# Feed-forward gate and value projections of one transformer layer as Strassen block products of seven terms

## What is computed

```python
def conv_ffn(h, P):
    u = depthwise_conv(h @ P['ffn_w_gate'], P['ffn_conv_w'], P['ffn_conv_b'])
    return (jax.nn.gelu(u, approximate=True) * (h @ P['ffn_w_val'])) @ P['ffn_w_down']

h = modulate(rms_norm(x, norm_ffn_pre[l]), sh2, sc2)     # h * (1 + scale) + shift
x = x + g2 * rms_norm(conv_ffn(h, P), norm_ffn_post[l])
```

## Time and profile before

| | us |
|---|---|
| median of 3 runs | 3854.72 (3853.71 to 3860.74) |
| the profiled execution | 3853.66 |
| its span, first to last instruction | 3851.9 |
| PE busy | 3631.2 (94%) |
| DVE busy | 1285.0 (33%) |
| ACT busy | 532.1 (14%) |

### The profile page before, as it was taken

The page is one execution under the profiler, slowest core; times in us unless marked ns, Lnnn a source line. Parts: engine busy times, 40 slices in busy tenths (PEclk is TensorE's granted clock), DMA queues, the critical chain, the costliest instruction groups (busy, mean ns, idle before and its releaser), DMA issues.

```text
span 3851.9 us, 43075 instructions
## 1 busy us (share of the span) xinstructions
PE 3631.2 (94%) x18490; PEld 2873.8 (75%) x18490; DVE 1285.0 (33%) x1928; ACT 532.1 (14%) x917; POOL 161.1 (4%) x166
## 2 busy tenths in 40 slices
PE   6999999978889899998999999999899979999979
PEld 2445475547778788887888888888788858888858
DVE  2257932236567410114212221000171251171260
ACT  1000012233344210010000000000101120101120
POOL 0000020000000100000000000000050000140000
PEclk9999999988889999999999999999899979999989
DMA  8868542013322434443444444444243303344303
GB/s 339 335 279 338 229 151 77 33 44 82 79 74 55 164 143 151 173 150 120 153 152 152 149 148 151 153 153 142 99 153 142 131 31 139 115 153 142 120 33 131
DMA packets 134143, 554.75 MB, mean 144 GB/s; under 512 B 57440, under 2 KB 61792, under 8 KB 72048
## 3 DMA queue, kind: packets, MB, share of 16 engines
q1 hardware_dynamic: 119680, 451.98, 33.6%
q10 hardware_dynamic: 14304, 100.42, 6.6%
HBM read 535.05 MB, written 17.30 MB: 143 GB/s over the span
## 4 chain that ended last, share of the span: by engine, by line
PE 69%; DVE 4%; ACT 2%; SPq 1%; DMA 1%; issue 1%; DVEq 0%; ACTq 0%
PE ps L435 58%; PE ps L1562 2%; PE ps L2819 1%; PE ps L1565 1%; PE ps L1660 1%; SPq L1383 1%; DVE arena L2007 1%; DVE arena L2009 1%; PE ps L2580 0%; DMA pack_t<-arena 0%; SPq L1386 0%; PE ps L2827 0%; PE ps L1439 0%; PE ps L1605 0%; PE ps L2575 0%
## 5 line engine op out<-in xcount | busy, mean ns | idle before, releaser
L435 PE MATMUL ps<-arena,ring 128*128 128x256 f32 (+3 forms) x11200 | 2586.4, 394 | 36.3 <-issue 15.7
L435 PEld LDWEIGHTS ps<-arena,ring 128*128 128x128 f32 (+1 forms) x11200 | 2136.4, 191 | 483.4 <-issue 189.7
L766 DVE SCALAR_TENSOR_TENSOR arena<-arena,small 128x512 f32<-128x512 f32 x240 | 180.4, 752 | 36.9 <-DMA arena<-in_ada_late 20.4
L2322 DVE TENSOR_TENSOR arena<-ps,arena 128x1024 f32<-128x1024 f32 x12 | 14.3, 1220 | 395.1 <-ACT arena L2308 395.1
L2699 DVE SCALAR_TENSOR_TENSOR arena<-arena,col 128x255 f32<-128x255 f32 (+29 forms) x180 | 108.2, 601 | 6.4
L570 PE MATMUL ps<-arena 128*128 128x512 f32 (+1 forms) x224 | 93.2, 565 | 5.3 <-ACT arena L631 5.3
L2443 DVE TENSOR_TENSOR arena<-ps,arena 128x1024 f32<-128x1024 f32 x11 | 13.5, 1224 | 239.2 <-PE ps L435 239.0
L2422 ACT ACT_TABLE_LOAD x11 | 14.1, 1283 | 535.0 <-DVE arena L2456 535.0
L2707 POOL TENSOR_TENSOR arena<-arena 128x1024 f32<-128x1024 f32 x2 | 4.7, 2350 | 1977.7 <-ACT arena L2648 1977.7
L570 PEld LDWEIGHTS ps<-arena 128*128 128x128 f32 x224 | 42.8, 199 | 56.3 <-issue 54.9
L1562 PE MATMUL ps<-arena 128*128 128x256 f32 x320 | 81.6, 411 | 1.0 <-ACT arena L1773 1.0
(11 more groups left out here) (419 smaller groups left out, 2969.1 us busy)
## 6 DMA issues: line engine op xcount, KB each, us to landing
ring<-in_weights SPq DMA_DIRECT2D x398, 1024.0 KB, 4.8
arena<-in_ada_late ACTq DMA_DIRECT2D x64, 1024.0 KB, 7.8
arena<-in_gates SPq DMA_DIRECT2D x56, 256.0 KB, 3.3
arena<-in_front ACTq DMA_DIRECT2D x8, 1024.0 KB, 8.9
arena<-in_x ACTq DMA_DIRECT2D x2, 2048.0 KB, 12.6
keep_g<-arena SPq DMA_DIRECT2D x14, 256.0 KB, 2.0
arena<-keep_h SPq DMA_DIRECT2D x3, 1024.0 KB, 7.8
arena<-in_ctx ACTq DMA_DIRECT2D x1, 2048.0 KB, 23.8
```

The costliest lines, as they stand in the source:

```text
L435: mm = M.matmul(o, ring[:, slot, k, c0:c0 + w], rhs, start=(kc == 0), stop=(kc == ktiles * WK - 1))
L766: ins = V.scalar_tensor_tensor(part[:, b], late[:, s, k], c, part[:, b], ALU.mult, ALU.add)
```

## The change

The first block of 512 gate and 512 value columns stays as it was, with 257 moving columns. The other ten blocks change.

Each weight tile of theirs now holds all 2048 inner rows of 128 output columns (`_chunk_tiles`), so two tiles are a matrix of 2048 x 256, which is cut in four quadrants: A11 and A12 (columns 0 to 127, rows 0 to 1023 and 1024 to 2047), A21 and A22 (the same of columns 128 to 255). The normalised input `h2` is cut in four as well: B11, B12 (tokens 0 to 127 and 128 to 255 of the first 1024 features), B21, B22. In place of the eight products of quadrants, seven are made (a form of Strassen's identity) of 8 matmuls with 128 moving columns each. A block of 512 gate and 512 value columns is four such pairs of tiles ("tile pairs" below), numbered 0 to 3: 0 and 1 are gate, 2 and 3 value; tile pairs take the PSUM halves in turn. That is 4 x 7 x 8 = 224 matmuls for each block, where 128 were.

- Once, before the loop: VectorE multiplies `hs` by `rs2` into `h2` (four instructions), ScalarE adds the shift (16 instructions), VectorE makes T1 to T4, the sums of quadrants of `h2`, and TensorE waits for T4 (`t_in4`) before its loop.
- For every tile pair VectorE makes S1 to S4 of the weights' quadrants (`weight_sums`: four instructions of 128x1024, after waiting for both tiles), in one of two buffers; TensorE waits for them (`s_in`) after its first three products, which use weights as they are.
- After every tile pair ScalarE copies the first product out of PSUM (`first_product`), and VectorE adds the products up to four quarters of the result (`quarters`: three instructions of 128x256 and one of 128x128), the last of which frees the PSUM half. This replaces the multiplication by `rs2` and the addition of the shift.
- `slot_left` is counted up at the first matmul of the first product (the second tile of the tile pair before is left) and at the first that reads S1 (the first tile of this one is left).
- The taps, the gelu and the gated product stay, from within the new order on VectorE.

```diff
+    gate, val = a['ffn_w_gate'][0], a['ffn_w_val'][0]
+    out += [_tiles(gate[:, 0:512]), _tiles(val[:, 0:512])]
+    gate, val = _chunk_tiles(gate[:, 512:]), _chunk_tiles(val[:, 512:])
...
+def _chunk_tiles(w):
+
+    return w.reshape(DC, P, -1, P).transpose(2, 1, 0, 3).reshape(-1, P, TILE)
...
+        HD = DC // 2
+        h2 = view(8192, DC, T)
...
+        PAIRS = 4
...
+        def pair_pe(p, half):
+
+            p.wait_ge(bf.free[half].sem, bf.free[half].due(p))
+            X, Y = ps[:, 4 * half], ps[:, 4 * half + 1]
+            S1, S2, S3, S4 = (S_SET[half][:, n] for n in range(4))
+
+            def product(o, w, x):
+                for k in range(HD):
+                    mm = M.matmul(o, w[:, k], x(k), start=(k == 0), stop=(k == HD - 1))
+                    if k == 0:
+                        first = mm
+                return first, mm
+            A11, A12 = quadrants(take_tile(p))
+            product(X[:, 0:P], A11, lambda k: h2[:, k, 0:P])[0].then_inc(slot_left.sem, slot_left.up(p))
+            product(X[:, P:2 * P], A12, lambda k: h2[:, HD + k, 0:P])
+            A21, A22 = quadrants(take_tile(p))
+            product(Y[:, 3 * P:4 * P], A22, lambda k: T4[:, k])
+            p.wait_ge(s_in.sem, s_in.due(p))
+            product(Y[:, 0:P], S1, lambda k: T1[:, k])[0].then_inc(slot_left.sem, slot_left.up(p))
+            product(Y[:, P:2 * P], S3, lambda k: T3[:, k])
+            product(X[:, 2 * P:3 * P], S2, lambda k: T2[:, k])
+            product(X[:, 3 * P:4 * P], S4, lambda k: h2[:, HD + k, P:T])[1].then_inc(bf.full[half].sem, bf.full[half].up(p))
+
         def ffn_pe(p):
...
-            pairs(p, FB - 1, 4, moving, bf)
+            p.wait_ge(t_in4.sem, 1)
...
+            with turns(p, FB - 1, {**per_tiles(2 * PAIRS), **bf.per(2), s_in: PAIRS}):
+                for j in range(PAIRS):
+                    pair_pe(p, j % 2)
...
+            def first_product(half):
+                a.wait_ge(bf.full[half].sem, bf.full[half].due(a))
+                S.copy(p1[:, half], ps[:, 4 * half, 0:P]).then_inc(p1_in.sem, p1_in.up(a))
...
+                first_product(0)
+                first_product(1)
+                gelus(i + 1)
+                first_product(0)
+                first_product(1)
             out_act(a)
...
+            def weight_sums(half):
+                a, b = ((ff_first[0] + 2 * half + n) % SLOTS for n in range(2))
+                for slot in (a, b):
+                    v.wait_ge(filled[slot].sem, filled[slot].due(v, 16))
+                (A11, A12), (A21, A22) = quadrants(a), quadrants(b)
+                S1, S2, S3, S4 = (S_SET[half][:, n] for n in range(4))
+                V.tensor_tensor(S1, A21, A22, ALU.add).then_inc(dve_step.sem, dve_step.up(v))
+                step(V.tensor_tensor(S3, A11, A21, ALU.subtract))
+                step(V.tensor_tensor(S2, S1, A11, ALU.subtract))
+                V.tensor_tensor(S4, A12, S2, ALU.subtract).then_inc(s_in.sem, s_in.up(v))
+
+            def quarters(dst, n, half):
...
+                v.wait_ge(p1_in.sem, p1_in.due(v))
+                step(V.tensor_tensor(q[:, 0:4:3], two(p1[:, half]), bank(0)[:, 1:3], ALU.add))
+                step(V.tensor_tensor(q[:, 1:3], two(q[:, 3]), bank(1)[:, 0:2], ALU.add))
+                V.tensor_tensor(q[:, 3], q[:, 2], bank(1)[:, 0], ALU.add).then_inc(dve_step.sem, dve_step.up(v))
                 v.wait_ge(dve_step.sem, dve_step.now(v))
...
+                step(V.tensor_tensor(q[:, 1:3], q[:, 1:3], ps[:, 4 * half:4 * half + 2, 3 * P:4 * P], ALU.add), bf.free[half])
...
+            for g in range(4):
+                V.tensor_tensor(h2[:, 4 * g:4 * g + 4], hs[:, 4 * g:4 * g + 4, 0:T], over(rs2, 4, T), ALU.mult)\
+                    .then_inc(h2_scaled.sem, h2_scaled.up(v))
+            whole(u, 0)
+            taps(0)
+            v.wait_ge(h2_in.sem, 1)
...
+            V.tensor_tensor(T4, B21, T2, ALU.subtract).then_inc(t_in4.sem, 1)
+            weight_sums(0)
+            whole(ct, 1)
+            gated(0)
+
+            def turn(i, more):
+                weight_sums(1)
+                quarters(u, 0, 0)
+                weight_sums(0)
+                quarters(u, 1, 1)
+                taps(i)
+                weight_sums(1)
+                quarters(ct, 0, 0)
+                if more:
+                    weight_sums(0)
+                quarters(ct, 1, 1)
+                gated(i)
```

More of the change, by code:

```diff
@@ L2397, in build_program, with quadrants @@
         conv_ready, gelu_ready, gv_in = again("ff_conv"), again("ff_gelu"), again("gv_in")
+        HD = DC // 2
+        h2 = view(8192, DC, T)
+        T1, T2, T3, T4 = view(13312, HD, P), view(14336, HD, P), view(15360, HD, P), view(40448, HD, P)
+        S_SET = [view(4096, 4, HD, P), view(36352, 4, HD, P)]
+        p1 = view(13056, 2, P)
+        h2_scaled, h2_in, t_in4 = again("h2_scaled"), again("h2_in"), again("t_in4")
+        s_in, p1_in = again("s_in"), again("p1_in")
+        PAIRS = 4
+        ff_first = [0]
+        def quadrants(slot):
+            w = ring[:, slot].rearrange("p k (a n) -> p (k a) n", n=P)
+            return w[:, 0:HD], w[:, HD:DC]
+        def pair_pe(p, half):
[18 more added lines that the diff above has]
+            product(X[:, 3 * P:4 * P], S4, lambda k: h2[:, HD + k, P:T])[1].then_inc(bf.full[half].sem, bf.full[half].up(p))
         def ffn_pe(p):
@@ L2407, in ffn_pe @@
             column_block(p, bf, 1, 4, moving, last_bank=lambda: wait(p, "var", 2))
-            pairs(p, FB - 1, 4, moving, bf)
+            p.wait_ge(t_in4.sem, 1)
+            ff_first[0] = tile_at[0] % SLOTS
+            ff_first[1:] = [f.count['wait', id(p)] for f in filled]
+            with turns(p, FB - 1, {**per_tiles(2 * PAIRS), **bf.per(2), s_in: PAIRS}):
+                for j in range(PAIRS):
+                    pair_pe(p, j % 2)
+            took(p, 2 * PAIRS, FB - 1)
             p.wait_ge(bf.free[0].sem, bf.free[0].due(p))
@@ L2418, in ffn_act, with gelus @@
             S.activation(rs2, rs2, ACT.Sqrt).then_inc(nb["root"].sem, nb["root"].up(a))
-            with turns(a, FB, {conv_ready: 1, gelu_ready: 1}) as i:
+            def gelus(i):
                 a.wait_ge(conv_ready.sem, conv_ready.due(a))
@@ L2424, in ffn_act @@
                 ins.then_inc(gelu_ready.sem, gelu_ready.up(a))
+            def first_product(half):
+                a.wait_ge(bf.full[half].sem, bf.full[half].due(a))
+                S.copy(p1[:, half], ps[:, 4 * half, 0:P]).then_inc(p1_in.sem, p1_in.up(a))
+            for c in range(DC):
+                if c % 4 == 0:
+                    a.wait_ge(h2_scaled.sem, c // 4 + 1)
+                ins = S.activation(h2[:, c], h2[:, c], ACT.Identity, bias=adac[:, 48 + c, 1:2])
+            ins.then_inc(h2_in.sem, 1)
+            gelus(0)
+            for h in range(2):
+                bf.full[h].due(a)
+            with turns(a, FB - 1, {conv_ready: 1, gelu_ready: 1, p1_in: PAIRS, bf.full[0]: 2, bf.full[1]: 2}) as i:
+                first_product(0)
[3 more added lines that the diff above has]
+                first_product(1)
             out_act(a)
@@ L2438, in ffn_dve, with step, taps @@
             variance(v, rs2, ps[:, 7, 0:T])
-            with turns(v, FB, {**bf.per(), conv_ready: 1, gelu_ready: 1, gv_in: 1, dve_step: 6}) as i:
+            def step(ins, ready=dve_step):
+                ins.then_inc(ready.sem, ready.up(v))
+                v.wait_ge(ready.sem, ready.now(v))
+            def taps(i):
                 tap = lambda j: K('conv_w', j * FC, FC)[:, bass.ds(i * 4, 4)].unsqueeze(2).to_broadcast([P, 4, T])
-                shift_of = lambda b: ps[:, b:b + 4, T:T + 1].to_broadcast([P, 4, T])
-                v.wait_ge(bf.full[0].sem, bf.full[0].due(v))
-                V.tensor_tensor(u[:], ps[:, 0:4, 0:T], over(rs2, 4, T), ALU.mult).then_inc(dve_step.sem, dve_step.up(v))
-                v.wait_ge(dve_step.sem, dve_step.now(v))
[L2445 to L2466, removed]
@@ new lines, in taps, with gated @@
+                V.tensor_tensor(cv[:], u[:], tap(1), ALU.mult).then_inc(dve_step.sem, dve_step.up(v))
+                step(V.tensor_tensor(ct[:], u[:], tap(0), ALU.mult))
+                step(V.tensor_tensor(cv[:, :, 1:T], cv[:, :, 1:T], ct[:, :, 0:T - 1], ALU.add))
+                step(V.tensor_tensor(ct[:], u[:], tap(2), ALU.mult))
+                step(V.tensor_tensor(cv[:, :, 0:T - 1], cv[:, :, 0:T - 1], ct[:, :, 1:T], ALU.add), conv_ready)
+            def gated(i):
+                v.wait_ge(gelu_ready.sem, gelu_ready.due(v))
+                step(V.tensor_tensor(gv[:, bass.ds(i * 4, 4), :], ge[:], ct[:], ALU.mult), gv_in)
@@ new lines, in whole @@
+            def whole(dst, half):
+                shift = ps[:, 4 * half:4 * half + 4, T:T + 1].to_broadcast([P, 4, T])
+                v.wait_ge(bf.full[half].sem, bf.full[half].due(v))
+                step(V.tensor_tensor(dst[:], ps[:, 4 * half:4 * half + 4, 0:T], over(rs2, 4, T), ALU.mult))
```

(18 more changed lines are left out.)

6 lines of the change are left out of this document (4 added, 2 removed).

## The result

The changed kernel takes 3797.12 us (median of 4 runs, 3795.69 to 3798.47) against 3854.22 for the one before on the same chip: 57.1 us less, a ratio of 0.985 (95% interval 0.9833 to 0.9867, which is 51 to 64 us less). The forecast was 3798.5.

What follows compares the result with a forecast made beforehand. TensorE (PE busy 94% of the span) was taken to bound the kernel. The ten blocks save 56.3 us, all other terms nothing: 3854.7 - 56.3 = 3798.4, forecast 3798.5 us, range 3788 to 3832.

Steps and rivals of the forecast that it cites:

- TensorE's sum: Ten changed blocks: 448 pairs at 111.7 ns, 50.04 us a block, 500.4 us against 556.7, 56.3 us less.
- The lower bound of 491.9 us: Ten changed blocks at 109.8 ns a pair, the spacing read from a burst with 64 columns: a gain of 64.8 us.
- Wait before the loop: Before the ten blocks: preparing the input and its sums lies beside the first value block and costs nothing; uncovered, 19 us once.
- VectorE in the loop: Ten changed blocks: VectorE's work, 37.5 us of 50.0 a block, fits; least slack 3.4 us, at tile pair 3.
- My sign of being right, DVE busy 35 to 38 us: In each changed block, VectorE's busy time was to show 35 to 38 us if the forecast held.
- Weights: Weight tiles in the loop: 168 GB/s, landing in 4.8 us; VectorE waits for the second tile, cost nothing.
- Tail: After the last block: the down projection wants block 10's gated product ten tiles later, so no cost.
- The loop's edge: TensorE's longer loop body: nothing taken; as a rival, an instruction fetch at 9 edges costs 18 us, 3816.5; chance 0.05.
- The slower rivals: Ten blocks' matmuls: low clock, up to 4306 us, chance 0.03; weight loads not hidden, up to 4158 us, chance 0.06.
- The doubt that I took from line 2580: Ten blocks' matmuls: narrow columns might lower the clock, as 16 columns showed 0.85 with TensorE busy; chance 0.03.
- VectorE late at tile pair 3: Rival: VectorE's sums for tile pair 3 overrun the 3.4 us slack; 3 us over is 30 us, 3828; chance 0.06.
- the clock only as a rival by itself: Ten blocks' matmuls: the clock at the low level, up to 225 ns a pair, all low 4306 us; chance 0.03.

Runs made afterwards that it cites:

- e1: Changed kernel with eight plain products in place of seven in the same tiles, no sums of weights or inputs: 3873.47 us.
- e3: Changed kernel with the seventh product of each tile pair, that with S4, left out: 3725.58 us.
- e7: Changed kernel with 64 moving columns in place of 128 in every matmul of the ten blocks: 3797.71 us.
- e2: Kernel before the change with only the rows normalised first, old blocks kept with 256 moving columns: 3854.17 us.
- e5: Changed kernel with the first sum for tile pair 3 (S1) repeated three more times on VectorE: 3797.71 us.
- e6: Changed kernel with the first sum for tile pair 3 (S1) repeated six more times on VectorE: 3852.08 us.
- e9: Changed kernel with five repeats of the first sum (S1) for tile pair 3 on VectorE: 3830.27 us.
- e8: Changed kernel with weights of 64 columns in place of 128 in every matmul of the ten blocks: 3788.13 us.
- e4: Changed kernel without the sums of weights and the waits for them; products read A21 and A22 instead: 3800.14 us.

## Why the prediction was right

- *TensorE's sum.* 448 x 111.7 = 50.04 us a block was forecast, 50.02 measured; 56.3 us of gain forecast, 556.7 - 500.2 = 56.5 in the stage (500.2 from first to last start), 57.1 by the medians. That the median came within 1.4 us of the forecast is partly luck, since its interval is some 6 us to either side; the stage's figure is the test. e1 and e3 changed the number of products by one either way, and both moved by 640 pairs at 111.67 ns (+71.5 in the loop and -71.5 us). That the load and not the columns sets it, e7 shows. The row that I had it from, line 1660, I read wrongly by 2 ns: the first two of its 32 pairs start 56 ns apart, all others 111 or 112, so 109.8 ns is the mean of a burst with an odd first step. The lower bound of 491.9 us that I built on it has no pair behind it; 64 columns cost 111.65 (e7).
- *Where the gain comes from.* The old form in halves of 128 columns would have cost 15.2 us (e1), the seventh product out of eight gives 71.5, together 56.3. The row normalised first, with nothing else, gives 4 us of the stage (e2), and is contained in the first step.
- *Wait before the loop.* `t_in4` was put 5.8 us ahead of need; T4 ends at 1821.8 us and TensorE's loop starts at 1828.56, 216 ns after the pair before. Right, with 6.8 us to spare.
- *VectorE in the loop.* 37.5 us a block forecast with its own waits. In the timeline above a set of sums takes 1862.32 to 1867.20, 4.9 us, the quarters 1.7, the taps 6.2: 34.0 us a block with the gated product, 32.6 of it instructions. I had charged every own wait 0.16 us, but most cost 0.03 to 0.04, and only some of those where the trace has a register instruction in front 0.14 to 0.19 (the one before line 2516: 0.17). The slack at tile pair 3 was 4.2 us where I had 3.4, elsewhere 7.5 (6.2 in the first block). e5 shows that the slack is real to within 0.4 us. My sign of being right, DVE busy 35 to 38 us, was not met (32.6): it counted waits as busy time.
- *Weights.* A tile lands in 4.8 us as before, with 168 GB/s, and VectorE's forecast wait for the second tile is there (2.85 us at 1871.6). It ends 5.5 us into the tile pair where I had 4.8, since the load is issued only some 0.6 us after the tile pair starts. Nobody waits for it.
- *Tail.* Nothing was taken: TensorE is not idle before any pair of line 442 between 1828 and 2460 us.
- *The loop's edge.* Nothing was taken, and the window over a whole block with an edge shows PE busy for 50.02 of 50.02. The Trainium skill's rule (Runtime: NRT & Kernel Launch, section Instruction fetch mechanics) that a branch beyond the pages held stalls for a fetch did not show as a cost at some 900 instructions either. The same section of the Trainium skill also gives TensorE a memory of 2048 instructions, in which the whole body would fit; the prediction left that out, and it could explain the missing cost. So could TensorE's queued work. No run here tells the two apart.
- *The slower rivals.* Weight loads hide in a stream of 4480 pairs as in a burst of 16. The Trainium skill's factor of 1.45 for a sustained stream (TensorE: Matmul & The Clock Gate, section Back-to-back issue gap) would have made it 162 ns; the trace has 111.67, so for fp32 pairs it does not hold here. (162 ns a pair would be 725.8 us for the ten blocks and a time of 4024, not the 4080 that I wrote.) The clock stayed at 1.00. The doubt that I took from line 2580 (16 columns, 0.85) concerns something real: its window splits into 1.00 up to 2752 us and 0.61 from there to 2755, with TensorE recorded as busy throughout. It did not happen with 128 columns, nor with 64 (e7).
- *VectorE late at tile pair 3.* Not met, but underpriced: I put an overrun at its own length, once a block. e6 shows 5.3 us a block for 3.4 us of overrun, since the clock goes down with it. The prediction had the clock only as a rival by itself, never as a part of the price of a wait.

## What to carry to other kernels

When the engine that bounds is full, price a rewrite of its work by the spacing of the nearest instructions already in the trace, not by their records' length (192 and 275 ns here, spacing 111.67) and not by the arithmetic saved. Take the spacing from single starts and not from the mean of a burst, whose first step can be odd.

The arithmetic alone misleads here: an eighth of the multiplications was worth a tenth of the stage, and only after the narrower matmuls had cost 15 us. Then lay the added work of the other engines out against each due time; the least slack, not the busy share, says how much more fits. And keep some of it: here ten idle times of 2.1 us cost 30 us in place of 21 (e9), and ten of 3.4 us cost 53 in place of 34 (e6).

## What the runs showed of the hardware

- An fp32 matmul is two pairs; at a clock of 1.00 a pair with full-width weights costs 111.67 ns with 128 moving columns, 111.65 with 64, 215.83 with 256 columns and 217.45 with 257; one with 64-wide weights and 128 columns costs 109.18 where all go to the same half of the partitions (e8).
- I had not expected the clock to turn on so little: with 2.1 us of idle time in front of work it fell to the low level (1.2 GHz, pairs at 213 ns) after five of ten waits, with 3.4 us after ten of ten, and each fall cost 1.6 to 3.1 us.
- VectorE writing 4 x 128 x 1024 values for every tile pair, into buffers that TensorE reads next, changes TensorE's pace by nothing that can be seen (e4 against the changed kernel: 500.4 and 500.4 us).
